# Token halves for the first feature tiles after seven block boundaries of a three-block transformer kernel

## The chip, the core and the metric

The kernel runs on one core of one Trainium2 chip, as one program. The metric is the device time of one execution in microseconds (us). Times of the trace are counted from the start of the span, the time from the first to the last instruction.

## The reference

Two blocks of a first model and one of a second run one after the other over x of 512 tokens by 1024 features, all in float32. What matters here is where a block's parts meet:

```
for i in range(2):
    m = even_mixer(x) if i % 2 == 0 else odd_mixer(x)      # attention
    x = layer_norm(ALPHA * x + m, ln1_g[i], ln1_b[i])
    x = layer_norm(ALPHA * x + square(relu(x @ w_up[i])) @ w_down[i], ln2_g[i], ln2_b[i])
    x = x + sigmoid(x @ ple_w_gate[i] + ple_b_gate[i]) * (p[i] @ ple_w_proj[i])
h = rmsnorm(x, norm1_g)                                    # gated linear attention, convolution
x = x + mixed(h)
h2 = rmsnorm(x, norm2_g)
x = x + (silu(h2 @ w_ffn_gate) * (h2 @ w_ffn_up)) @ w_ffn_down
return rmsnorm(x, norm_f_g)
```

## The kernel before, in words

**Products.** Every float32 product is made of three products of rounded parts (type fp32r): high by high, high by low, low by high (`mm3`). Weights come as 301 chunks of 128 x 1024, in the order of `STAGES`. SP loads a chunk into RW (four buffers). POOL's `cut` makes its high part WH (L532) and then its low part WL (L535), in two buffers each, when TensorE has used the chunk two before (`chunk_used`). TensorE waits for `lo_split` before it uses a chunk. The activations lie with features on partitions as 8 tiles k of 128 x 512 tokens: XTH (high) and XTL (low).

**Order of the work.** Each engine runs one list written by hand, and semaphores join the lists. A projection runs over k = 0 to 7 outermost (two k to a chunk); in `features` each k has 4 column groups of 3 matmuls of 512 columns, into four PSUM banks.

**Boundaries.** Eight places, b = 0 to 7, stand where a block's part ends and a norm (or, at b = 2, nothing but the sum) comes between it and the next projection. `BOUND[b]` is (residual is added, kind of norm, number of its gains). Boundaries 0, 1, 3, 4 are "layer", 6 and 7 are "rms" with an addition, 2 has no norm and 5 is "rms" without an addition, these two behind an embedding stage. At a boundary with an addition four token tiles t of 128 x 1024 go through:

- VectorE (DVE, `boundary`): residual(t) (L1588 or L1593, from PSUM), then scale(t-1) one tile later: reciprocal L1599, then L1605 (layer) or L1609 (rms). Its order is residual 0, 1, scale 0, residual 2, scale 1, residual 3, scale 2, scale 3.
- ScalarE (ACT, `boundary`): deviation(t), the squares L2107 or L2110 and the root L2111; then copy_out(t), L2118, which brings the turned tile from PSUM to YT (in the profile: HT), the last tile in two halves of features; then gain and bias for k = 1 to 7 (L2139, L2142) over all 512 tokens.
- TensorE (PE, `boundary`): 8 transposes (L894) of each tile; between them `occupy` fills waits with matmuls on a tile of ones whose results nobody reads.
- DVE again: for each k over all 512 tokens the gain and bias of k = 0 (L1629, L1632), the high part (L1637) and the low part (L1638), which counts `xt_ready`; after the last k the residual tiles get gain and bias (L1572, L1573).

TensorE then starts the next projection at k = 0: `hidden` (boundaries 0, 3, 6), `embedding` and its `gate_half` (1, 4), or `features` (2, 5). At 1 and 4 `embed_tile`, a product that needs nothing of the norm, is run between the transposes.

**Other places touched.** `forget_sums` (L1200 and L1201): four float32 matmuls of 512 columns into one bank. The last boundary, b = 7: scale is L1613, and SP stores each tile of out by one DMA of 512 KB (L519). Some operands of the third block (QIH to STL, GLH, TWH, OH and their low parts) start 128 or 192 bytes behind a multiple of 256 bytes in a partition, which follows from the sizes of what is placed before them.

Of the kernel before, what the change touches and what calls it, by code (L numbers as in the profile page):

```python
# [81 lines left out]
FOX0 = 16  # L82

# [91 lines left out]
def program(nc, d, out):  # L175
    ctx = ExitStack()
    with ctx:
# [19 lines left out]
        IDLE = sb("IDLE", [P, P], F32R)  # L197
        EPS = sb("EPS", [P, 2])
# [28 lines left out]
        _pad = sb("PAD_PREPARE", [P, 8], at=prepare)  # L227
# [76 lines left out]
        _pad = sb("PAD_THIRD", [P, 8], at=third)  # L304
# [19 lines left out]
        DEC = sb("DEC", [P, 2, NCH], at=third)  # L324
        ST = sb("ST", [P, 2, 2 * DV], at=third)
# [6 lines left out]
        ORS = sb("ORS", [P, GLA_H], at=third)  # L332
        decays = ExitStack()
# [24 lines left out]
        def turned_at(b, t):  # L358


            return (t if BOUND[b][0] else (t + 2) % T) * D

        def probs(h):
# [121 lines left out]
                 (True, "layer", 3), (False, "rms", 4), (True, "rms", 5), (True, "rms", 6)]  # L485
        Y_BASE = [0, 4, 8, 12, 16, 20, 20, 20]

        @block.sync
        def _(sp):
# [30 lines left out]
            sp.wait_ge(out_stored, 16 * T)  # L520
# [3 lines left out]
        def _(pool):  # L524
            own = Order(pool, pool_own)

            def cut(i, j):
# [6 lines left out]
                pool.wait_ge(hi_split, 2 * (j + 1) + 2 * RAW * i)  # L534
                pool.tensor_tensor(WL[:, j % WS, :], RW[:, j % RAW, :], WH[:, j % WS, :].bitcast(F32),  # L535
# [76 lines left out]
            over_chunks(pool, FIRST["out0"] + WS - 1, c + 3, cut)  # L612
# [27 lines left out]
            over_chunks(pool, FIRST["out1"] + WS - 1, CHUNKS, cut)  # L640
# [3 lines left out]
        def _(pe):  # L644
# [20 lines left out]
            def features(c, bank, r=0, new=0, freed=None, late=None, steps=None):  # L665
# [4 lines left out]
                for k in range(k_tiles):  # L670
                    cc, u = c + k // 2, UNIT * (k % 2)
                    if new:
                        pe.wait_ge(xt_ready, KD * (new - 1) + k + 1)
                    if k % 2 == 0:
                        chunk(cc, r)
                    for m, col in enumerate(columns):
                        if freed is not None and k == 0:
                            pe.wait_ge(mix_out, freed + m + 1)
                        if late is not None and k == 0 and m == 3:
                            pe.wait_ge(yt_copied, late)  # L680
# [9 lines left out]
            def tokens(c, bank, h=XTH, l=XTL, k_tiles=KD, new=0, steps=None, freed=None):  # L690

                for k in range(k_tiles):
                    cc, u = c + k // 2, UNIT * (k % 2)
                    if new:
# [214 lines left out]
            def hidden(c, groups, g0, new):  # L909
# [8 lines left out]
                for g in range(n):  # L918
                    one(g, 0)
# [1480 lines left out]
```

## Time and profile before

| | us |
|---|---|
| median of 3 runs | 1978.86 (1978.25 to 1979.53) |
| the profiled execution, its own time | 1978.09 |
| its span | 1976.3 |
| mean granted TensorE clock | 0.998 |
| busy: PE, PEld | 1947.2, 1616.1 |
| busy: POOL, DVE, ACT | 1261.1, 868.8, 327.0 |

PE is TensorE's matmuls, PEld its weight loads, which overlap them. The profiled execution's time is 1.8 us above its span and 0.8 us below the median. Fill matmuls (`occupy`, operand IDLE) count as busy PE: 152 records, 42.4 us.

### The profile page before, as it was taken

How to read it: one execution, taken by the hardware profiler on the slowest of the kernel's cores; microseconds unless marked ns; L12 is line 12 of the kernel's file. 1: busy time of each engine (PE TensorE's matmuls, PEld its weight loads, DVE VectorE, ACT ScalarE, POOL GpSimd, SP SyncE). 2: the span in 40 equal slices, each digit the busy share in tenths (PEclk: the TensorE clock that was granted, in tenths of full speed). 3: DMA queues.
4: the chain of work that ended last, by engine and by line, in shares of the span. 5: the costliest groups of instructions: out<-in, count | busy, mean ns of one | idle time of the engine just before them, and what ended most of it. 6: DMA issues, size and time to landing. Idle time of an engine off the chain costs nothing.

```text
span 1976.3 us, 24552 instructions
## 1 busy us (share of the span) xinstructions
PE 1947.2 (99%) x9180; PEld 1616.1 (82%) x9180; DVE 868.8 (44%) x1208; ACT 327.0 (17%) x627; POOL 1261.1 (64%) x818
## 2 busy tenths in 40 slices
PE   9999999999999999999999999999999999999998
PEld 8788788888887878888788888877888788888886
DVE  3587372253349511472832343377457840000234
ACT  1377300000003100462300000033122130000001
POOL 5586576667767547775566677756453556666674
PEclk9999999999999999999999999999999999999999
DMA  6410233333332323112233333322222233333332
GB/s 225 131 33 33 85 107 96 96 96 117 96 96 85 97 69 108 60 54 79 72 121 99 99 116 98 96 84 88 67 86 65 75 94 98 96 96 96 96 96 75
DMA packets 53698, 181.31 MB, mean 92 GB/s; under 512 B 6584, under 2 KB 9322, under 8 KB 53498
## 3 DMA queue, kind: packets, MB, share of 16 engines
q1 hardware_dynamic: 46656, 165.17, 26.8%
q10 hardware_dynamic: 6970, 15.11, 2.2%
q8 instruction: 53, 0.87, 0.2%
q14 instruction: 19, 0.16, 0.0%
HBM read 176.56 MB, written 3.70 MB: 91 GB/s over the span
## 4 chain that ended last, share of the span: by engine, by line
PE 90%; DVE 4%; POOL 3%; ACT 1%; issue 1%; POOLq 0%; DVEq 0%
PE PS L646 87%; POOL WL L535 1%; PE PS L815 1%; PE PS L894 1%; POOL WH L532 1%; POOL PB L563 1%; DVE STL L1871 0%; DVE X L1605 0%; DVE PS L1588 0%; DVE STH L1870 0%; DVE ST L1880 0%; DVE U L1933 0%; ACT HT L2107 0%; ACT PTH L2058 0%; DVE PTL L1518 0%
## 5 line engine op out<-in xcount | busy, mean ns | idle before, releaser
L535 POOL TENSOR_TENSOR WL<-RW,WH 128x1024 fp32r<-128x1024 f32 x301 | 762.7, 2534 | 25.1
L532 POOL TENSOR_SCALAR WH<-RW 128x1024 fp32r<-128x1024 f32 x301 | 351.7, 1169 | 628.0 <-PE PS L646 603.5
L646 PE MATMUL PS<-XTH,WH 128*128 128x512 f32 x1168 | 457.3, 392 | 2.1 <-DVE XTL L1638 1.6
L646 PE MATMUL PS<-XTL,WH 128*128 128x512 f32 x1168 | 455.4, 390 | 0.0
L646 PE MATMUL PS<-XTH,WL 128*128 128x512 f32 x1168 | 455.3, 390 | 0.0
L646 PE MATMUL PS<-WL,HSH 128*128 128x512 f32 x688 | 267.6, 390 | 2.1 <-POOL WL L535 2.1
L646 PE MATMUL PS<-WH,HSL 128*128 128x512 f32 x688 | 267.7, 389 | 0.0
L646 PE MATMUL PS<-WH,HSH 128*128 128x512 f32 x688 | 267.6, 389 | 0.0
L646 PEld LDWEIGHTS PS<-XTH,WH 128*128 128x128 f32 x1168 | 219.7, 188 | 50.9 <-DVE XTL L1638 3.7
L646 PEld LDWEIGHTS PS<-XTH,WL 128*128 128x128 f32 x1168 | 219.7, 188 | 45.9
L646 PEld LDWEIGHTS PS<-XTL,WH 128*128 128x128 f32 x1168 | 219.6, 188 | 44.0
L646 PE MATMUL PS<-WH,XTH 128*128 128x512 f32 (+1 forms) x480 | 182.7, 385 | 1.5 <-POOL WL L535 0.9
L646 PE MATMUL PS<-WL,XTH 128*128 128x512 f32 (+1 forms) x480 | 181.3, 383 | 0.5 <-POOL WL L535 0.5
L646 PE MATMUL PS<-WH,XTL 128*128 128x512 f32 (+1 forms) x480 | 181.6, 382 | 0.0
L1691 DVE CAST HSH<-HT 128x512 fp32r (+1 forms) x86 | 40.3, 468 | 273.8 <-PE PS L646 273.0
L646 PEld LDWEIGHTS PS<-WL,HSH 128*128 128x128 f32 x688 | 128.9, 188 | 30.0 <-POOL WL L535 3.4
L646 PEld LDWEIGHTS PS<-WH,HSL 128*128 128x128 f32 x688 | 129.2, 188 | 26.9
L646 PEld LDWEIGHTS PS<-WH,HSH 128*128 128x128 f32 x688 | 129.2, 188 | 26.8
L1653 DVE TENSOR_SCALAR HT<-PS 128x2048 f32 (+1 forms) x16 | 36.7, 2292 | 202.2 <-PE PS L646 201.5
L1692 DVE TENSOR_TENSOR HSL<-HT,HSH 128x512 fp32r<-128x512 f32 x86 | 124.0, 1442 | 3.0
L646 PEld LDWEIGHTS PS<-WH,XTH 128*128 128x128 f32 x480 | 90.0, 188 | 22.2 <-issue 4.6
L1675 DVE TENSOR_TENSOR HT<-PS,GT 128x1024 f32 (+1 forms) x11 | 13.5, 1225 | 214.7 <-ACT GT L2270 214.7
(337 smaller groups left out, 2304.7 us busy)
## 6 DMA issues: line engine op xcount, KB each, us to landing
RW<-stream SPq DMA_DIRECT2D x302, 512.0 KB, 3.6
BC<-gate_rows SPq DMA_DIRECT2D x16, 256.0 KB, 3.2
G<-gain_rows ACTq DMA_DIRECT2D x5, 512.0 KB, 3.7
X<-x ACTq DMA_DIRECT2D x1, 2048.0 KB, 11.1
G<-bias_vecs ACTq DMA_DIRECT2D x4, 512.0 KB, 5.2
out<-X SPq DMA_DIRECT2D x4, 512.0 KB, 2.7
XS<-xt ACTq DMA_DIRECT2D x3, 512.0 KB, 8.3
bias_rows<-QM ACTq DMA_DIRECT2D x1, 1536.0 KB, 6.8
```

The source lines that it names most:

```text
L532: pool.tensor_scalar(WH[:, j % WS, :], RW[:, j % RAW, :], 1.0, 1.0, ALU.mult, ALU.mult).then_inc(hi_split, 1)
L535: pool.tensor_tensor(WL[:, j % WS, :], RW[:, j % RAW, :], WH[:, j % WS, :].bitcast(F32), ALU.subtract).then_inc(lo_split, 1)
L563: x = pool.tensor_scalar(p, p, SM[:, s, i:i + 1], 1.0, ALU.mult, ALU.mult)
L646: return pe.matmul(o, a, b, start=start, stop=stop)
L815: x = pe.transpose(PSF[:, o:o + P], probs(h)[:, p:p + P], IDENT[:, :])
L894: x = pe.transpose(PSF[:, o:o + P], src[:, k * P:(k + 1) * P], IDENT[:, :])
L1653: ve.tensor_scalar(h, PS[:, 4 * (g % 2):4 * (g % 2) + 4, :], 0.0, None, MAX).then_inc(relued, 1)
L1675: ve.tensor_tensor(h, PS[:, bank + 2:bank + 4, :], GT[:, :, :], M).then_inc(relued, 1)
L1691: own(ve.tensor_copy(HSH[:, k % 2, :], h))
L1692: ve.tensor_tensor(HSL[:, k % 2, :], h, HSH[:, k % 2, :].bitcast(F32), SUB).then_inc(hs_ready, 1)
```

## The change

It touches all seven boundaries before b = 7, that last one, and the places of some operands:

- The first three feature tiles (k = 0, 1, 2) behind a boundary are made in two halves of 256 tokens. TensorE begins with the half of tokens 0 to 255 before token tile 3 is normed; it turns tile 3 between these products. The four banks are first set to zero by a matmul with a tile of zeros (`clear`), and all products add to them. (`gate_half` needs no `clear`, since its token tiles have banks of their own.)
- ScalarE, not VectorE, makes the high part of k = 3 to 7 at boundaries with a norm.
- VectorE's scale(3) comes after the first half's splits: after all three, at "rms" after two, and after one at boundaries 1 and 4.
- POOL's low part of the second chunk behind a boundary waits until VectorE has made the third tile's first half. ScalarE copies out tiles 0 and 1 before deviation(3).
- Of the fill matmuls three stay at boundaries with an addition and no embedding, eight at b = 5.
- At b = 0, 3, 5, 7 a root of a spare element is taken by ScalarE before the first deviation. The last tile of out is scaled and stored in two halves.
- In `forget_sums` the columns that are zero are left out: 512, 384, 256 and 128 columns.
- Pads put the operands of the third block on multiples of 256 bytes.

```diff
+SPLIT_K = 3
+HALVES = (slice(0, S // 2), slice(S // 2, S))
+def ready_parts(b, k, half):
+    base = KD + (KD + SPLIT_K) * b
+    return base + (half * SPLIT_K + k + 1 if k < SPLIT_K else SPLIT_K + k + 1)
...
-        _pad = sb("PAD_THIRD", [P, 8], at=third)
+        _pad = sb("PAD_U", [P, 40], at=third)
...
+        _pad = sb("PAD_DEC", [P, 48], at=third)
...
+        _pad = sb("PAD_ORS", [P, 16], at=third)
...
-            return (t if BOUND[b][0] else (t + 2) % T) * D
+            return (t if BOUND[b][0] else t % 2 + 2) * D
...
-            for t in range(T):
-                sp.wait_ge(y_ready, Y_BASE[7] + t + 1)
-                sp.dma_start(out[:, t, :], X[:, t, :]).then_inc(out_stored, 16)
+            ends = [(t, slice(0, D)) for t in range(T - 1)] + [(T - 1, half) for half in OUT_HALVES]
+            for j, (t, w) in enumerate(ends):
+                sp.wait_ge(y_ready, Y_BASE[7] + j + 1)
+                sp.dma_start(out[:, t, w], X[:, t, w]).then_inc(out_stored, 16)
...
                 pool.wait_ge(hi_split, 2 * (j + 1) + 2 * RAW * i)
+                if b is not None:
+                    pool.wait_ge(xt_ready, ready_parts(b, SPLIT_K - 1, 0))
                 pool.tensor_tensor(WL[:, j % WS, :], RW[:, j % RAW, :], WH[:, j % WS, :].bitcast(F32),
...
+            cut_stages(FIRST["out0"] + WS - 1, ((0, "up0"), (1, "ple0"), (2, "fox")), c + 3)
...
+            cut_stages(FIRST["out1"] + WS - 1, ((3, "up1"), (4, "ple1"), (5, "gla"), (6, "ffn")), CHUNKS)
...
+            def clear(bank):
+                mm(PS[:, bank, :].rearrange("p (t n) -> p t n", t=T), ZERO[:, :],
+                   IDLE[:, :].unsqueeze(1).to_broadcast([P, T, P]), True, False)
+            def first_group(c, b, turn_tile):
+                def one(k, half):
...
+                    pe.wait_ge(xt_ready, ready_parts(b, k, half or 0))
+                    for m in range(4):
+                        w = slice(u + m * P, u + (m + 1) * P)
+                        x = mm3(PS[:, m, ts], WH[:, cc % WS, w], WL[:, cc % WS, w],
+                                XTH[:, k, ts], XTL[:, k, ts], False, k == KD - 1)
+                    return x
+                chunk(c)
+                one(0, 0)
+                if not BOUND[b][0]:
+                    turn_tile(T - 1)
+                one(1, 0)
+                if BOUND[b][0]:
+                    turn_tile(T - 1)
+                chunk(c + 1)
+                one(2, 0)
+                one(0, 1)
+                one(1, 1).then_inc(chunk_used, 1)
+                one(2, 1)
+                for k in range(SPLIT_K, KD):
...
             def boundary(b, c, embed=None):
                 add, kind, n = BOUND[b]
                 if kind and not add:
                     pe.wait_ge(emb_z, 16)
                     occupy(4, 8)
+                    pe.wait_ge(var_ready, 4 * n + T)
+                    for bank in range(T):
+                        clear(bank)
+                turn_tile(b, 0)
+                turn_tile(b, 1)
                 if embed:
+                    pe.wait_ge(yt_copied, 5 * b + 1)
+                    embed(0)
+                    embed(1)
+                    turn_tile(b, 2)
+                    pe.wait_ge(yt_copied, 5 * b + 2)
+                    embed(2)
+                    turn_tile(b, T - 1)
+                    embed(3)
+                    return
+                if add:
+                    pe.wait_ge(yt_copied, 5 * b + 1)
+                    occupy(0, 3)
+                elif not kind:
+                    pe.wait_ge(y_ready, Y_BASE[b] + T)
...
+                turn_tile(b, 2)
+                first_group(c, b, lambda t: turn_tile(b, t))
...
                for t in range(T):
-                    mm(PS[0:RANK, 4, :], LF[:, RANK * t:RANK * (t + 1)],
-                       STEPS[:, 3 * P - t * P:3 * P - t * P + S], t == 0, t == T - 1)
+                    mm(PS[0:RANK, 4, t * P:], LF[:, RANK * t:RANK * (t + 1)],
+                       STEPS[:, 3 * P:3 * P + S - t * P], t == 0, t == T - 1)
...
+                    last_at = 1 if embedding_layer is not None else 2 if kind == "rms" else SPLIT_K
+                    for k in range(SPLIT_K + 1):
+                        if kind and add and k == last_at:
+                            scale(3)
+                        if k < SPLIT_K:
+                            split_half(k, 0)
+                    for k in range(SPLIT_K):
+                        split_half(k, 1)
+                    for k in range(SPLIT_K, KD):
...
+                        split(k)
...
+                if kind and b in (0, 3, 5, 7):
+                    act.activation(SPARE[:, 0:1], EPS[:, 0:1], F.Sqrt)
+                ahead = T if b == 7 or not add else T - 1
+                if kind:
+                    for t in range(ahead):
+                        deviation(t)
+                if b < 7:
+                    copy_out(0)
+                    copy_out(1)
+                if kind and ahead < T:
+                    deviation(T - 1)
...
+                        for k in range(1, SPLIT_K):
+                            features_ready(k, HALVES[0])
+                    copy_out(2)
                     copy_out(T - 1, slice(0, KD // 2))
...
+                        for k in range(1, SPLIT_K):
+                            features_ready(k, HALVES[1])
+                        features_ready(SPLIT_K)
+                    copy_out(T - 1, slice(KD // 2, KD))
...
+                        for k in range(SPLIT_K + 1, KD):
+                            features_ready(k)
```

`split(k, ts)` is the old work of one k on DVE (k = 0: gain and bias; the high part where k < 3 or at b = 2; the low part), over the tokens ts; `features_ready(k, ts)` is ACT's gain and bias and, from k = 3 on, its copy into XTH. The old loops that these replace are gone.

## Rows read from the trace of the kernel before

**Rows 1.** The page: busy time by engine, and the chain by engine.
```profile
PE 1947.2 (99%) x9180; PEld 1616.1 (82%) x9180; DVE 868.8 (44%) x1208; ACT 327.0 (17%) x627; POOL 1261.1 (64%) x818
...
PE 90%; DVE 4%; POOL 3%; ACT 1%; issue 1%; POOLq 0%; DVEq 0%
```

**Rows 2.** Windows, boundaries 0, 1, 2, 5, 6: last product to next (columns: first row).
```profile
core 0: us, PE busy (x) PEld busy (x) DVE busy (x) ACT busy (x) POOL busy (x), PEclk, DMA share, GB/s
234.20:244.35 10.15, 8.41 (x50) 6.26 (x49) 7.95 (x16) 8.15 (x13) 5.71 (x3) 1.00 0.32 103
594.00:605.46 11.46, 11.14 (x64) 8.79 (x62) 8.69 (x15) 9.59 (x16) 5.72 (x4) 1.00 0.29 92
655.70:661.73 6.03, 5.74 (x41) 5.06 (x42) 3.06 (x6) 3.82 (x5) 3.42 (x2) 1.00 0.37 110
...
1371.70:1385.66 13.96, 11.36 (x65) 9.17 (x65) 8.42 (x15) 10.68 (x18) 3.42 (x2) 1.00 0.20 70
1598.60:1607.19 8.59, 8.04 (x53) 6.49 (x50) 6.59 (x9) 6.86 (x12) 6.89 (x4) 1.00 0.25 67
```

**Rows 3.** Timeline of boundary 0: start us, us, engine, line, operation [idle before].
```profile
230.23 1.28 ACT L2111 ACT_TABLE_LOAD   x1
...
239.41 1.34 DVE L1605 TENSOR_SCALAR X<-PS,MV,RSTD 128x1024 f32<-128x1024 f32 x1
...
241.94 0.59 ACT L2118 COPY HT<-PS 128x512 f32<-128x512 f32 x1 [0.68 <-PE PS L894]
242.56 0.82 ACT L2139 ACTIVATE HT<-HT,BIASES,GAINS 128x512 f32<-128x512 f32 x1
242.56 0.55 DVE L1629 TENSOR_SCALAR HT<-HT,GAINS,BIASES 128x512 f32<-128x512 f32 x1 [1.81 <-ACT HT L2118]
243.14 0.43 DVE L1637 CAST XTH<-HT 128x512 fp32r<-128x512 f32 x1
...
243.60 0.69 DVE L1638 TENSOR_TENSOR XTL<-HT,XTH 128x512 fp32r<-128x512 f32 x1
```

**Rows 4.** Timeline of TensorE (PE) in the third block: matmuls of 256 columns.
```profile
1487.20 0.28 PE L646 MATMUL PS<-STL,QEH 128*128 128x256 f32 x1
1487.32 0.28 PE L646 MATMUL PS<-STH,QEL 128*128 128x256 f32 x1
```

**Rows 5.** Timeline behind boundary 1: POOL's and DVE's low parts side by side.
```profile
606.58 2.44 POOL L535 TENSOR_TENSOR WL<-RW,WH 128x1024 fp32r<-128x1024 f32 x1
606.81 2.76 DVE L1638 TENSOR_TENSOR XTL<-HT,XTH 128x512 fp32r<-128x512 f32 x1
```

**Rows 6.** Timeline of boundary 5.
```profile
1373.09 2.37 POOL L535 TENSOR_TENSOR WL<-RW,WH 128x1024 fp32r<-128x1024 f32 x1
1373.69 2.32 DVE L1715 TENSOR_SCALAR HT<-X,RSTD 128x1024 f32<-128x1024 f32 x1
...
1376.07 1.09 PE L894 MATMUL PS<-IDENT,HT 128*128 128x128 f32 x8 [2.18 <-DVE HT L1715]
```

**Rows 7.** Timeline of the last boundary: the table load, the root behind it, the last scale.
```profile
1963.18 1.28 ACT L2111 ACT_TABLE_LOAD   x1
1964.48 0.29 ACT L2111 ACTIVATE STD<-MV,EPS 128x1 f32<-128x1 f32 x1
...
1971.68 1.28 DVE L1613 SCALAR_TENSOR_TENSOR X<-X,RSTD,G 128x1024 f32<-128x1024 f32 x1
```

**Rows 8.** The page: the four stores of out.
```profile
out<-X SPq DMA_DIRECT2D x4, 512.0 KB, 2.7
```

**Rows 9.** Timeline of TensorE (PE): forget_sums.
```profile
722.37 3.61 PE L646 MATMUL PS<-STEPS,LF 128*16 128x512 f32 x8
```

**Rows 10.** Windows of products: inside a projection, with OH, with XTH (columns as rows 2).
```profile
300.00:334.00 34.00, 34.00 (x152) 28.16 (x151) 7.71 (x3) 0.00 (x0) 22.06 (x14) 1.00 0.31 100
...
1557.96:1574.56 16.60, 16.60 (x71) 13.49 (x72) 16.36 (x13) 1.96 (x4) 11.20 (x6) 1.00 0.30 95
1576.20:1590.00 13.80, 13.80 (x62) 11.43 (x61) 2.00 (x3) 0.62 (x1) 9.78 (x6) 1.00 0.36 112
```

More of the change, by code:

```diff
@@ L972, in one @@
                                k == 0, k == KD - 1)
-                for k in range(KD - 2):
-                    if new:
-                        pe.wait_ge(xt_ready, KD * (new - 1) + k + 1)
+                if b is not None:
+                    pe.wait_ge(yt_copied, 5 * b + 3)
+                    for half in range(2):
+                        if half:
+                            pe.wait_ge(yt_copied, 5 * b + 5)
+                        for k in range(SPLIT_K):
+                            if k % 2 == 0 and not half:
+                                chunk(c + k // 2)
+                            pe.wait_ge(xt_ready, ready_parts(b, k, half))
+                            for t in (2 * half, 2 * half + 1):
+                                x = one(k, t)
+                            if k == 1 and half:
+                                x.then_inc(chunk_used, 1)
+                for k in range(0 if b is None else SPLIT_K, KD - 2):
+                    if b is not None:
+                        pe.wait_ge(xt_ready, ready_parts(b, k, 0))
                     if k % 2 == 0:
@@ L984, in gate_half @@
                         x.then_inc(chunk_used, 1)
[L985 to L986 removed]
+                if b is not None:
+                    pe.wait_ge(xt_ready, ready_parts(b, KD - 1, 0))
                 chunk(c + 3)
@@ new lines, in split @@
+                def split(k, ts=slice(0, S)):
+                    y = YT[:, k, ts]
+                    if k == 0 and layer:
+                        own(ve.tensor_scalar(y, y, GAINS[:, n, 0:1], BIASES[:, n, 0:1], M, A))
+                    elif k == 0 and kind:
+                        own(ve.tensor_scalar(y, y, GAINS[:, n, 0:1], None, M))
+                    if k < SPLIT_K or not kind:
+                        own(ve.tensor_copy(XTH[:, k, ts], y))
+                    ve.tensor_tensor(XTL[:, k, ts], y, XTH[:, k, ts].bitcast(F32), SUB).then_inc(xt_ready, 1)
@@ new lines, in split_half @@
+                def split_half(k, half):
+                    if k and kind:
+                        ve.wait_ge(yt_ready, (KD + SPLIT_K - 2) * n + (SPLIT_K - 1) * half + k)
+                    else:
+                        ve.wait_ge(yt_copied, 5 * b + 2 + 2 * half)
+                    split(k, HALVES[half])
+                if kind:
+                    residual(0)
+                    residual(1)
+                    if add:
+                        scale(0)
+                    residual(2)
+                    if add:
+                        scale(1)
+                    residual(3)
+                    if add:
+                        scale(2)
+                    if b == 7 or not add:
+                        scale(3)
```

196 lines of the change are left out of this document (87 added, 109 removed).

## The prediction

> **What bounds the kernel now.** I read the page first. TensorE is busy for 99% of the span and POOL, the next, for 64%; the chain that ended last runs through TensorE for 90% [rows 1]. So an edit pays only where TensorE waits, fills, or multiplies what need not be multiplied. Those places are the boundaries. In windows from the last product of one part to the first of the next, 10.15 us pass at boundary 0, 11.46 at 1, 6.03 at 2, 13.96 at 5 and 8.59 at 6 [rows 2]; 3 goes like 0 (10.09) and 4 like 1 (11.45). The busy time in those windows is mostly fill, transposes (four times 1.09 [rows 6]) and, at 1 and 4, the embedding product. The timeline of boundary 0 says which wait ends last: scale 3 on DVE (1.34), transposes, half a copy (0.59), gain (0.55), high part (0.43), low part (0.69) [rows 3], and the first product starts at 244.35. All of tile 3 has to pass before any product starts. At boundary 5 two more things show: a DVE scale that took 2.32 beside POOL's low part of 2.37, and TensorE idle for 2.18 until it was done [rows 6].
>
> **Prices.** Half a feature tile on DVE: the whole takes 0.55, 0.43 and 0.69 [rows 3]; a half costs at least half of that and at most all. I take 0.35, 0.28 and 0.42, near the lower end, since length sets most of such an operation. So k = 0 costs 1.15 with gaps, k = 1 and 2 cost 0.75 each. ACT's half gain: 0.5 of 0.82 [rows 3]. ACT's high part of 512 columns: never seen here; between the copy's 0.59 and the gain's 0.82 [rows 3], I take 0.62. Products of 256 columns: two starts lie 0.12 us apart [rows 4], 0.115 over a longer stretch, against 0.227 for 512 columns (34.00 us for 150 of them, two of the 152 counted lying across the edges [rows 10]); twice the weight loads cost next to nothing (72 half products a boundary, 0.1 to 0.2). Twelve such products, one k of one half, are 1.4 us. `clear` and the three fills take 0.23 each in time in which TensorE waits anyway.
>
> **Boundaries 0 and 3.** The table load of 1.28 stands between the squares of tile 0 and their root [rows 3]; scale 0 waits for it, and residual 2 and all that follows on DVE stand behind scale 0. With the root taken ahead, in idle time of ACT, I put 1.15 of it on the path (0 if something else held DVE; at most 1.28). Scale 2, which ended a little before scale 3's 239.41, would then end near 238.0. New order: DVE's first half of k = 0 until 239.15, k = 1 until 240.1 (behind deviation 3 on ACT), k = 2 until 240.9; TensorE starts at 239.2, 5.1 earlier than now. Then it waits for more: scale 3 ends at 242.4, tile 3 is turned by 243.4; POOL's low part of the second chunk, released at 240.9, takes 2.4 and ends at 243.3; k = 2, first half, runs until 244.8; the copy, gain and split of the second half of k = 0 are done at 245.2. So TensorE waits about 0.4, and the three k end at 249.4. Now the same 36 products of 0.227 end at 252.5. Gain 3.1 each. Later k are covered: ACT needs about 1.5 for a k (gain, then high part), TensorE 2.7. The next cut of POOL is released earlier than now (second half of k = 1, at 248.0) and is needed at 252.1.
>
> **A rule against the trace.** ACT starts its next instruction 1.30 after the load's start [rows 7], so a removed load is worth at most 1.3 here. The Trainium skill, ScalarE: Activation LUTs, section What ACT_TABLE_LOAD costs, adds a drain and makes a switch 2.66 us; by that page the three loads on the path (b = 0, 3, 7) would give some 4 us more. No row shows the drain, and my sum goes by 1.3.
>
> **Boundaries 1 and 4.** The table is loaded already. Half 0 is split at about 601.9, since scale 3 comes after its first k. But here the second chunk is the first that `gate_half` uses: TensorE can't start before POOL's low part ends, 601.9 + 2.4 = 604.3, against 605.46. Then POOL cuts the next chunk at once (until 607.9), TensorE needs it at 607.1 for k = 2, and DVE's second half is caught beside it: an operation of 0.69 became 2.76 beside POOL's 2.44 [rows 5]. Start 1.1 earlier, stall 0.8: gain 0.2 each, bounds -1.5 and +1.1.
>
> **Boundary 2.** No norm. TensorE begins after two copies instead of four, 659.9 instead of 661.73, turns tile 3 (1.1) in between, and waits for POOL from the first half's 661.4 until 663.8. End of the three k: 669.4 against 669.9. Gain 0.5.
>
> **Boundary 5.** POOL's low part, which now held DVE from 1373.69 to 1376.01 [rows 6], comes after the splits: four scales of 0.8 end at 1377.1. The fills between the turns go, and turns 0 to 2 need no deviation beside them. ACT finishes its deviations at 1376.1 (load gone), copies 0 and 1 by 1378.15; first product at 1379.35 against 1385.66. Turn of tile 3, POOL until 1383.25, second half ready by 1384.4: the three k end at 1388.8 against 1393.9. Gain 5.1, the largest term; bounds 3 (DVE's halves locked behind POOL once) and 6.
>
> **Boundary 6.** No load here, and the first chunk's cut still holds scale 2. First product at 1603.95 against 1607.19, POOL until 1608.9, end 1614.5 against 1615.4. Gain 0.9.
>
> **The end.** The load of 1.28 [rows 7] holds scale 0 and so residuals 2 and 3: 0.9 of it counts, as tile 3's sums are then the limit. Last scale 1.28 [rows 7]: two halves of about 0.68. A store of 512 KB takes 2.7 to land [rows 8]; of 256 KB, started 0.1 later than the old one relative to the scale, I take 2.0 (bounds 1.4 and 2.7). Gain 0.9 + 0.6, with less queueing behind tile 2's store: 1.7, bounds 0.9 and 2.3.
>
> **Sums, places, start.** The four float32 matmuls of 2048 columns take about 3.55 until the next group [rows 9]; 1280 columns take 2.2: gain 1.3, as TensorE is bound there. The 72 products with OH start 0.234 apart, those with XTH behind them 0.230 and elsewhere 0.227 [rows 10]. If the place of the operand is the reason, 96 products with OH and 24 with TWH give 0.4 to 0.8: I take 0.6, bounds 0 and 1.5, since smaller operands may gain too. The memset of ZERO stands behind that of IDLE, and TensorE waits for both before its first fill: 0.1 lost. The DMAs on ACT's queue (forget and gate weights) start with the last `xt_ready` as before; they have no new wait. DVE's gains and biases of the residual start no later than now.
>
> **Sum.** 2 x 3.1 + 2 x 0.2 + 0.5 + 5.1 + 0.9 = 13.1; with 1.7, 1.3, 0.6 and -0.1: 16.6. The profiled execution, 1978.1, goes to 1961.5; it stands 0.8 below the median, so the median goes from 1978.9 to **1962.3**.
>
> **Rivals.**
> 1. *The head start is given back.* TensorE starts early and then stands before the second half, because scale 3, turn, copy and split of tile 3 are now behind more work. Against it: I find only 0.4 of such waiting. For it: DVE has 2.2 of half splits ahead of scale 3 at boundaries 0 and 3. Then boundaries 0 and 3 give only the load (1.2 each), 5 gives 3.5, 6 and 2 nothing: 5.9, with the 3.5 of other terms 9.4. Time 1969.5. Chance 0.16.
> 2. *POOL's new wait becomes the bound.* The low part of 2.4 [rows 6] is released by DVE and awaited by TensorE, with slack near zero at all seven; half of it, 1.2, lost at each is 8.4. Time 1970.7. Chance 0.12.
> 3. *Slower: the clock falls.* Some 120 fill matmuls go, and TensorE waits uncovered for up to 1 us several times in a boundary. For it: less activity. Against it: it stood idle for 2.18 at boundary 5 [rows 6] in a window whose granted clock is 1.00 [rows 2]. At the lower level (1.2 instead of 2.4 GHz) each product of 0.227 takes as much again; it becomes slower overall from 16.6 / 7 = 2.4 us a boundary, some 11 products at the low level after each. At 20 products, 4.5 x 7 = 32 lost: 1994. Chance 0.03. The Trainium skill, TensorE: Matmul & The Clock Gate, section HAM oscillation, says that gaps between bursts of matmuls can bring the clock down again and again; by that rule this case would come about, and no row of this kernel has shown it so far.
> 4. *The change doesn't do what it says* (both 1 and 2, the load still in the path, places without effect): 1 to 4 gained, about 1976. Chance 0.07.
>
> **How the numbers follow.** My forecast has 0.62. Its own terms leave 1958 to 1966. The range takes rivals 1 and 2 in and leaves out 3 and 4: 1957 to 1971. A measurement of this kernel can tell about 0.2%, 4 us, from no change: faster is the forecast and rivals 1 and 2 (0.90), less what may fall short, 0.89; same 0.08; slower 0.03.
>
> **What would show it.** Right: no table load between squares and root at boundaries 0, 3 and 7; first product near 239.3 at boundary 0 and a group of 12 matmuls of 256 columns 0.115 apart; TensorE's wait for DVE's second half at most 0.5; at boundary 5 scales of 0.75, none of 2.3; the low part of POOL ending when k = 1 and turn 3 end. Wrong: idle before TensorE's k = 2 with POOL L535 as releaser, over 1 us; DVE's half splits of over 1 us beside POOL; products 0.4 apart behind a boundary, or a granted clock below 0.99.

## The result, and the profile after

The changed kernel took 1963.76 us (median of 4, 1961.73 to 1965.80) beside 1978.55 for the kernel before (median of 4, 1978.11 to 1979.53): ratio 0.9924, 95% interval 0.9912 to 0.9936, 14.8 us faster. Forecast were 1962.3 and a range of 1957 to 1971. The profiled execution took 1963.95, its span is 1962.0 against 1976.3.

Page of the changed kernel, busy time by engine, beside [rows 1]:

```profile
PE 1932.6 (99%) x9287; PEld 1612.3 (82%) x9287; DVE 869.2 (44%) x1228; ACT 349.7 (18%) x673; POOL 1262.0 (64%) x818
```

TensorE's busy time fell by 14.6, all but 0.3 of which shows in the span (14.3). ACT took over 22.7 us of work, DVE's hardly changed: the high parts went, the gaps and locks of halves came.

Windows from the last product of one part to the first of the next, boundaries 0, 1, 2, 5, 6 of the changed kernel, as [rows 2]:

```profile
core 0: us, PE busy (x) PEld busy (x) DVE busy (x) ACT busy (x) POOL busy (x), PEclk, DMA share, GB/s
233.91:238.75 4.84, 4.70 (x31) 3.65 (x30) 4.55 (x9) 4.72 (x10) 3.35 (x2) 1.00 0.27 69
591.05:601.30 10.25, 9.45 (x57) 7.61 (x55) 8.34 (x16) 7.92 (x15) 5.73 (x4) 1.00 0.14 51
652.80:657.14 4.34, 3.75 (x30) 3.34 (x29) 2.76 (x6) 2.18 (x3) 1.04 (x1) 1.00 0.27 101
1365.34:1372.70 7.36, 5.82 (x36) 4.78 (x37) 6.40 (x15) 7.23 (x15) 1.07 (x1) 1.00 0.13 52
1586.73:1592.03 5.30, 4.51 (x32) 3.71 (x30) 5.16 (x7) 4.41 (x9) 4.14 (x3) 1.00 0.24 65
```

The first product comes 5.3, 1.2, 1.7, 6.6 and 3.3 us sooner. That isn't the gain: token tile 3 is now turned behind the first product, and new waits may lie there. So I measure stretches instead, from the start of the last product ahead of one boundary to that ahead of the next (the last one to the end of the span). Each holds one boundary with all that it drags behind it:

| stretch, us | before | after | gain | forecast |
|---|---|---|---|---|
| boundary 0 to 1 | 359.76 | 357.14 | 2.6 | 3.1 |
| 1 to 2 | 61.75 | 61.76 | 0.0 | 0.2 |
| 2 to 3 (with forget_sums) | 294.05 | 292.60 | 1.5 | 0.5 + 1.3 |
| 3 to 4 | 360.24 | 357.07 | 3.2 | 3.1 |
| 4 to 5 | 61.69 | 62.87 | -1.2 | 0.2 |
| 5 to 6 (with OH, TWH) | 226.95 | 221.39 | 5.6 | 5.1 + 0.6 |
| 6 to the end | 378.08 | 375.66 | 2.4 | 0.9 + 1.7 |

Two of the seven, 1 and 4, gave nothing or lost. Now the timelines, beginning with boundary 0 of the changed kernel (engines merged, by start):

```profile
236.15 1.34 DVE L1693 TENSOR_SCALAR X<-PS,MV,RSTD 128x1024 f32<-128x1024 f32 x1
237.41 0.41 DVE L1713 TENSOR_SCALAR HT<-HT,GAINS,BIASES 128x256 f32<-128x256 f32 x1
237.85 0.29 DVE L1717 CAST XTH<-HT 128x256 fp32r<-128x256 f32 x1
238.18 0.43 DVE L1718 TENSOR_TENSOR XTL<-HT,XTH 128x256 fp32r<-128x256 f32 x1
...
240.38 2.39 POOL L556 TENSOR_TENSOR WL<-RW,WH 128x1024 fp32r<-128x1024 f32 x1 [3.12 <-DVE XTL L1718]
241.74 1.09 PE L946 MATMUL PS<-IDENT,X 128*128 128x128 f32 x8
244.75 0.39 PE L677 MATMUL PS<-XTH,WH 128*128 128x256 f32 x1 [0.24 <-DVE XTL L1718]
...
245.32 0.62 ACT L2247 CAST XTH<-HT 128x512 fp32r<-128x512 f32 x1
```

A half costs 0.41, 0.29 and 0.43, where 0.35, 0.28 and 0.42 were taken; ACT's high part costs 0.62, as taken. TensorE starts at 238.75 and waits 0.24 for the second half. POOL's low part stands right behind the first half's last split. On DVE only scale 3 runs beside it, which reads PSUM: it takes 1.35 there (from 240.34), as it does with POOL idle (1.34, in the run without POOL's wait below). The scale of boundary 5, which reads SBUF, was the one that took 2.32.

Boundary 5, beside [rows 6]: no scale of 2.32 any more, and POOL's low part starts 3.3 us behind the last scale's end:

```profile
1367.37 0.75 DVE L1832 TENSOR_SCALAR HT<-X,RSTD 128x1024 f32<-128x1024 f32 x1
...
1369.95 0.75 DVE L1697 TENSOR_SCALAR HT<-X,RSTD 128x1024 f32<-128x1024 f32 x1
1372.70 0.36 PE L677 MATMUL PS<-XTH,WH 128*128 128x256 f32 x1 [1.03 <-DVE XTL L1718]
1374.04 2.39 POOL L556 TENSOR_TENSOR WL<-RW,WH 128x1024 fp32r<-128x1024 f32 x1 [7.35 <-DVE XTL L1718]
```

Boundary 1, where nothing was won: DVE and POOL, and TensorE's wait for each chunk:

```profile
601.33 1.14 DVE L1717 CAST XTH<-HT 128x256 fp32r<-128x256 f32 x1
602.41 2.38 POOL L556 TENSOR_TENSOR WL<-RW,WH 128x1024 fp32r<-128x1024 f32 x1
602.51 2.57 DVE L1718 TENSOR_TENSOR XTL<-HT,XTH 128x256 fp32r<-128x256 f32 x1
...
609.44 1.05 POOL L550 TENSOR_SCALAR WH<-RW 128x1024 fp32r<-128x1024 f32 x1 [4.64 <-PE PS L677]
609.48 2.09 DVE L1660 TENSOR_TENSOR X<-X,G 128x1024 f32<-128x1024 f32 x1
610.58 3.23 POOL L556 TENSOR_TENSOR WL<-RW,WH 128x1024 fp32r<-128x1024 f32 x1
```

POOL's second low part makes the chunk for k = 2 ready at 604.79: TensorE's wait there is 0.57 (forecast 0.8). But POOL's next cut begins only when k = 1 of both halves is multiplied, 609.44, and by then DVE has the residual's gain and bias (L1660, L1661). The low part takes 3.23, and TensorE waits 0.63 more, for k = 4. At boundary 4 the same two waits are 0.77 and 1.47:

```profile
1320.91 1.22 DVE L1660 TENSOR_TENSOR X<-X,G 128x1024 f32<-128x1024 f32 x1
1321.13 1.91 POOL L550 TENSOR_SCALAR WH<-RW 128x1024 fp32r<-128x1024 f32 x1 [4.67 <-PE PS L677]
1322.16 1.95 DVE L1661 TENSOR_TENSOR X<-X,G 128x1024 f32<-128x1024 f32 x1
1323.13 3.21 POOL L556 TENSOR_TENSOR WL<-RW,WH 128x1024 fp32r<-128x1024 f32 x1
```

The end, beside [rows 7]: no table load, the last residual starts 0.04 behind TensorE's last product, and the two halves of the last scale take 1.41. From that product's end (1954.90) to the end of the span it is 7.1; before it was 8.7.

```profile
1954.94 1.22 DVE L1681 SCALAR_TENSOR_TENSOR X<-X,PS 128x1024 f32<-128x1024 f32 x1
1957.37 0.29 ACT L2228 ACTIVATE STD<-MV,EPS 128x1 f32<-128x1 f32 x1
1957.90 1.41 DVE L1702 SCALAR_TENSOR_TENSOR X<-X,RSTD,G 128x512 f32<-128x512 f32 x2
```

Products with OH in the changed kernel, 72 in 16.46 where [rows 10] have 71 in 16.60; over all 96 the starts within a run lie 0.2273 apart, before 0.2325:

```profile
1546.54:1563.00 16.46, 16.46 (x72) 13.62 (x73) 16.21 (x13) 1.96 (x4) 11.51 (x6) 1.00 0.33 96
```

### The profile page after: what moved, and what is told of

Read it like the earlier page. It is cut to its first block and busy times, and to the rows that moved or that the text cites. A ratio compares the mean times of both kernels' runs of the same rounds, so it can differ in the third digit from the quotient of the medians.

```text
span 1962.0 us, 24847 instructions
## 1 busy us (share of the span) xinstructions
PE 1932.6 (99%) x9287; PEld 1612.3 (82%) x9287; DVE 869.2 (44%) x1228; ACT 349.7 (18%) x673; POOL 1262.0 (64%) x818
## 5 line engine op out<-in xcount | busy, mean ns | idle before, releaser
L677 PE MATMUL PS<-XTH,WH 128*128 128x512 f32 (+1 forms) x1228 | 469.1, 382 | 3.9 <-DVE XTL L1718 2.3
L677 PE MATMUL PS<-XTH,WL 128*128 128x512 f32 (+1 forms) x1228 | 466.0, 379 | 0.0
L677 PE MATMUL PS<-XTL,WH 128*128 128x512 f32 (+1 forms) x1228 | 465.9, 379 | 0.0
L677 PEld LDWEIGHTS PS<-XTH,WH 128*128 128x128 f32 x1228 | 231.3, 188 | 51.3 <-POOL WL L556 3.8
L677 PEld LDWEIGHTS PS<-XTH,WL 128*128 128x128 f32 x1228 | 231.2, 188 | 43.6
L677 PEld LDWEIGHTS PS<-XTL,WH 128*128 128x128 f32 x1228 | 231.4, 188 | 42.1
```

Source lines behind the costliest of these rows:

```text
L677: return pe.matmul(o, a, b, start=start, stop=stop)
```

## The experiments

Twelve runs were made, each beside the kernel before, the first of them with the changed kernel itself. Where no other is named, the measure for a time is the changed kernel at 1963.6 to 1963.8.

**The changed kernel again** (no edit), to learn how far its stretches repeat.

> The changed kernel once more, on the chip that also runs the next three. Theory: 1963.8 us again, and the stretch from the last product before boundary 4 to the last before boundary 5 takes 62.9 us again, with two waits for POOL's low part (0.77 and 1.47 us), since DVE's gain and bias of the residual (0.8 us apart from the next cut in the first trace) slow POOL's third cut. Rival: that stretch was a chance of one execution and is 61.8 us, as at boundary 1, in this one.

Measured: 1963.61 (1961.78 to 1964.84), ratio 0.9925 (0.9908 to 0.9941). The stretch behind boundary 4 is 62.88 again, with the same two waits (0.79 and 1.52), as the theory had it. Six of the seven stretches agree within 0.13 with the first profile. The seventh, 2 to 3, is 290.97 instead of 292.60; the clock section below tells why.

**Without the spare root ahead**, at b = 0, 3, 5, 7:

```diff
-                if kind and b in (0, 3, 5, 7):
-                    act.activation(SPARE[:, 0:1], EPS[:, 0:1], F.Sqrt)
```

> The changed kernel without the root of a spare element taken ahead, so that the table load of 1.28 us is back behind the first squares of boundaries 0, 3 and 7. Theory (the load delays scale 0 and all that stands behind it on DVE): first products of boundaries 0 and 3 come 1.1 to 1.2 us later, the end 0.9 us later, together 3.2 us slower than the changed kernel. Rival A (the halves hide it): less than 1 us. Rival B (a switch costs 2.66 us by the Trainium skill, ScalarE: Activation LUTs, section What ACT_TABLE_LOAD costs): 7 us.

**Only the root ahead**, the same two lines added to the kernel before:

> The kernel before, with one edit: the spare root ahead at b = 0, 3, 5, 7. Theory (a table load between squares and root delays scale 0 by 1.2 wherever ACT's deviations lead): boundaries 0 and 3 give 1.2 each, the end 0.9, 3.3 together, and boundary 5 nothing, since there DVE's scale of 2.32 beside POOL ends last: 1975.3. Rival A (at boundary 5 too, as in the changed kernel, where leaving the root out cost 1.2): 4.5 faster, 1974.1. Rival B (the load was hidden at 0 and 3 in the kernel before, and only the new order brings it onto the path): 0.9 faster, 1977.7.

Measured: without it 1969.64 (1967.05 to 1970.87), ratio 0.9955 (0.9938 to 0.9971), 6.0 slower, nearly twice the 3.2 of the theory. The stretches behind 0, 3 and 5 grow by 1.4, 1.2 and 1.2, the end by 1.1, which makes 4.9 (boundary 5 was not in the theory); 1.1 more is behind boundary 1, where POOL is caught for longer. So the total comes near Rival B's 7, but no single place shows its 2.66. Alone on the kernel before it gave 1974.56 (1972.29 to 1976.21), ratio 0.9976 (0.9964 to 0.9987), 4.3 faster: 1.3 at 0, 1.3 at 3, 1.4 at the end (4.0 together) and nothing at 5 (227.01 against 226.95). So a load is on the path wherever ACT leads, at 1.1 to 1.4 each. At boundary 5 of the kernel before it was hidden by the locked DVE scale, which is there still:

```profile
1371.47 2.32 DVE L1716 TENSOR_SCALAR HT<-X,RSTD 128x1024 f32<-128x1024 f32 x1
```

Once POOL's low part is out of its way, the load would be late there too: the two edits share that gain. The timeline of ACT without the root, boundary 0:

```profile
230.34 1.28 ACT L2228 ACT_TABLE_LOAD   x1
231.63 0.29 ACT L2228 ACTIVATE STD<-MV,EPS 128x1 f32<-128x1 f32 x1
```

The next instruction starts 1.29 behind the load's start. The Trainium skill, ScalarE: Activation LUTs, section What ACT_TABLE_LOAD costs, has 1283 ns for the load, as here, and a drain that makes the switch 2.66 us. The trace doesn't show the drain in this place, and four places of at most 1.4 speak against it.

**POOL's low part not held back**, at any boundary:

```diff
-                if b is not None:
-                    pool.wait_ge(xt_ready, ready_parts(b, SPLIT_K - 1, 0))
```

> The changed kernel without POOL's wait for DVE's first half before the low part of the second chunk, at all seven boundaries. Theory (DVE and POOL exclude each other, so the low part must not lie in DVE's splits): at boundary 5 a scale of 2.3 us instead of 0.75 returns and the first product comes 1.3 to 1.6 us later; at 0 and 3 the low part ends at about 239 instead of 242.8 and holds DVE's first half by 1.3 to 2 us, so that the first product is 1.5 us later, and about 0.5 us of it is won back at the third feature tile; at 1 and 4 nothing, as the low part ends before the embedding product does in either case. Sum 2 to 4 us slower. Rival (POOL's wait is the new bound): 2 to 5 us faster, since TensorE no longer waits for the second chunk.

Measured: 1975.86 (1973.73 to 1978.12), ratio 0.9986 (0.9977 to 0.9996): 12 slower, three times what I expected. At boundary 0 POOL's low part now starts 0.09 before DVE's first half, and DVE stands:

```profile
237.43 2.37 POOL L553 TENSOR_TENSOR WL<-RW,WH 128x1024 fp32r<-128x1024 f32 x1
237.52 2.42 DVE L1710 TENSOR_SCALAR HT<-HT,GAINS,BIASES 128x256 f32<-128x256 f32 x1
```

0.41 became 2.42, and all that follows on DVE is 2.0 late: the stretches grow by 1.9 at 0, 1.9 at 1, 3.4 at 3, 0.8 at 4, 1.4 at 5 and 2.0 at 6. This one wait of POOL carries most of what the change brings. At boundary 3 a fall of the clock is in it: TensorE stands for 2.14, and the windows around and behind that have the clock at 0.73 and 0.92. But at boundary 6 of the same execution it stands for 2.65, its longest wait at a boundary, and the clock stays at 1.00:

```profile
956.56 0.36 PE L674 MATMUL PS<-XTH,WH 128*128 128x256 f32 x1 [2.14 <-DVE XTL L1715]
...
1604.01 0.36 PE L674 MATMUL PS<-XTH,WH 128*128 128x256 f32 x1 [2.65 <-DVE XTL L1715]
```

```profile
955.00:960.00 5.00, 3.44 (x19) 3.47 (x20) 4.02 (x9) 0.90 (x1) 0.48 (x1) 0.73 0.39 117
960.00:965.00 5.00, 4.52 (x35) 4.31 (x35) 2.18 (x7) 2.87 (x5) 0.00 (x0) 0.92 0.00 0
1604.00:1610.00 6.00, 5.57 (x45) 5.37 (x46) 3.22 (x10) 1.95 (x4) 0.00 (x0) 1.00 0.23 87
```

Back to the two rows of boundary 0. The Trainium skill, SBUF — State Buffer, section SBUF: two separate sides, says that the ports which VectorE's faster operations, or those with two SBUF inputs, share with GpSimd are an exclusive lock: whoever starts first has them for the whole instruction, and the other blocks. The rows agree: DVE ends at 239.94, 0.14 after POOL's 239.80, and POOL is not slowed (2.37), rather than both going at half speed.

**DVE makes the high parts again** for k = 3 to 7, ACT only the gains:

```diff
-                    if k < SPLIT_K or not kind:
-                        own(ve.tensor_copy(XTH[:, k, ts], y))
+                    own(ve.tensor_copy(XTH[:, k, ts], y))
```

> The changed kernel, but DVE makes the high part of k = 3 to 7 again, ACT only the gains. Theory (that part of the change gives nothing by itself: DVE needs 0.43 + 0.69 = 1.1 us for a k, ACT 0.8, and TensorE 2.7): 0 plus or minus 0.5, 1963.6. Rival A (DVE's high parts push its low parts into POOL's cuts, where 0.69 becomes 2.76, and the next k is late): idle of TensorE before k = 3 or 4 of up to 1 us at boundaries 0, 3, 5 and 6, 2 to 4 us slower, 1966 to 1968. Rival B (ACT's gain followed by its high part and an extra pass is the slower way, and k = 3 comes sooner without): up to 1 us faster.

Measured: 1964.12 (1963.29 to 1964.62), ratio 0.9925 (0.9909 to 0.9942): no difference, as the theory had it. The stretches of boundaries 0, 3, 5 and 6 are within 0.25 of those of the changed kernel. At 1 and 4 the wait for k = 4 is gone, since DVE comes later to the residual, and another comes further on: TensorE stands 1.17 and 1.69 for DVE's embedding work (tile SG).

**Without the last fills** at boundaries 0, 3, 5, 6:

```diff
-                    occupy(4, 8)
...
-                    occupy(0, 3)
```

> The changed kernel without the fill matmuls that are left at the boundaries (three at 0, 3, 6, eight at 5), so that TensorE waits with nothing to do. Theory (the waits there don't bring the clock down): the granted clock at every boundary stays 1.00, products behind it 0.115 and 0.227 apart, 0 plus or minus 0.3 us, 1963.6. Rival (the fills are what holds the clock): a granted clock of 0.5 in a stretch behind boundary 5, or behind 0 and 3 as well, with products twice as far apart; 20 such products cost 2.3 to 4.5 us a boundary, 1966 to 1980.

Measured: 1965.96 (1963.05 to 1966.16), ratio 0.993 (0.9913 to 0.9946). The boundaries are the same to 0.1 (stretches 357.21, 357.16, 221.42, 375.52), at a granted clock of 1.00 in all of them, though TensorE now stands for 2.06 at boundary 5. That the median is 2 higher isn't from there: in the profile 1.1 is boundary 1 (62.86 instead of 61.8) and 1.6 the fall of the clock behind forget_sums.

**The three small parts undone**: forget_sums, pads and last store as before (the three pads are put back as well):

```diff
-                    mm(PS[0:RANK, 4, t * P:], LF[:, RANK * t:RANK * (t + 1)],
-                       STEPS[:, 3 * P:3 * P + S - t * P], t == 0, t == T - 1)
+                    mm(PS[0:RANK, 4, :], LF[:, RANK * t:RANK * (t + 1)],
+                       STEPS[:, 3 * P - t * P:3 * P - t * P + S], t == 0, t == T - 1)
...
-        OUT_HALVES = (slice(0, UNIT), slice(UNIT, D))
+        OUT_HALVES = (slice(0, D),)
```

> The changed kernel with its three small parts outside the halves undone: forget_sums over 512 columns in all four matmuls, the pads as before, the last tile of out scaled and stored whole. The trace of the changed kernel shows the 96 products with OH at 0.2273 us apart instead of 0.2325 and the 24 with TWH at 0.2270 instead of 0.2326 (0.6 us together), and a span that ends 7.1 us behind the last product instead of 8.7. Theory (each small part is worth what its rows say): 1.3 (sums) + 0.6 (places) + 0.6 (last store) = 2.5 us slower, 1966.1; the stretch from boundary 2 to 3 longer by 1.3, that from 5 to 6 by 0.6, with the pitch of OH back at 0.232 to 0.234. Rival A (the place of the operand has nothing to do with the pitch, which came from something beside it): pitch stays at 0.227, 1.9 slower. Rival B (the last store is hidden behind that of tile 2): the end keeps its 7.1, again about 1.9 slower, told apart from A by the stretch.

Measured: 1965.76 (1965.31 to 1968.30), ratio 0.9932 (0.9916 to 0.9949), 2.0 to 2.2 slower. The stretch 2 to 3 grows by 1.2. The OH products go back to 0.2325 apart, the TWH ones too (from 0.227 to 0.2327), on the same data and beside the same work, so the place is the reason; by pitch that is 0.6, though the stretch 5 to 6 shows only 0.4. The end behind the last product grows from 7.1 to 7.3: within the span the last store in halves is worth 0.3, not the 0.6 I had put. Outside it, the time stands 2.3 to 2.4 above the span in all four executions of this kernel, beside 1.8 to 2.0 in those of every other; no trace shows why.

**Another order of the gate product** at boundaries 1 and 4: k = 0 and 1 of both halves, and then k = 2, so that the first chunk is freed before k = 2 begins:

```diff
-                    for half in range(2):
-                        if half:
+                    for k, half in ((0, 0), (1, 0), (0, 1), (1, 1), (2, 0), (2, 1)):
+                        if k == 0 and half:
```

> The changed kernel with another order of the first gate products at boundaries 1 and 4: both halves of k = 0 and 1, then both of k = 2, so that the first gate chunk is used up before the next is begun. Theory (the halves' order asks for the second gate chunk 2.7 us after the start instead of 5.4, and frees the first 1.4 us later, so that the third chunk's cut falls into DVE's gain and bias): the waits for POOL (0.57 and 0.63 at boundary 1, 0.77 and 1.47 at 4) go, and one wait of about 1.1 us for DVE's second half comes; boundary 1 within 0.3 us, boundary 4 1.0 us faster; sum 1.0 us. Rival (POOL is slow there whatever the order, as DVE's gain and bias run beside it): no difference.

Measured: 1959.88 (1959.03 to 1962.33), ratio 0.9905 (0.9888 to 0.9921), 3.8 faster. The stretches are 60.37 (from 61.8) and 61.70 (from 62.9). At boundary 1 all waits for POOL behind the first product are gone; at boundary 4 one of 0.95 is left, for DVE:

```profile
1313.48 2.40 POOL L556 TENSOR_TENSOR WL<-RW,WH 128x1024 fp32r<-128x1024 f32 x1
1313.58 2.58 DVE L1717 TENSOR_TENSOR XTL<-HT,XTH 128x256 fp32r<-128x256 f32 x1
```

POOL came 0.10 ahead of DVE, and the second half of k = 0 was late. At boundary 1 of the same execution DVE's same part began first (602.78, POOL's at 603.73) and ended at 603.92; the lock then fell on the next k's high part (2.50), for which nobody waited. Which of the two is first differs between boundaries and executions of one kernel: in the combined version below boundary 1 has the wait and 4 has not. The two stretches make 2.6 of the 3.8; for the rest no place shows. Part of it may be the clock: three of these four executions have a mean granted clock of 0.999, but only four of the eight of the changed kernel.

**The same order, and POOL free at boundaries 1 and 4:**

```diff
-            cut_stages(FIRST["out0"] + WS - 1, ((0, "up0"), (1, "ple0"), (2, "fox")), c + 3)
+            cut_stages(FIRST["out0"] + WS - 1, ((0, "up0"), (2, "fox")), c + 3)
...
-            cut_stages(FIRST["out1"] + WS - 1, ((3, "up1"), (4, "ple1"), (5, "gla"), (6, "ffn")), CHUNKS)
+            cut_stages(FIRST["out1"] + WS - 1, ((3, "up1"), (5, "gla"), (6, "ffn")), CHUNKS)
```

> The version with the new order of the gate product (k0 and k1 of both halves first), and POOL's low part behind boundaries 1 and 4 not held back any more. Theory (POOL's wait earns its time there too, since a free low part lies beside DVE's scale or first half split): the first product of the gate comes 0.8 later as in the run without any such wait, at 1 and 4 each, 1.6 us slower than the new order alone: 1961.5. Rival (with the new order the wait only delays POOL, whose low part ends last before the first product there): 0.5 faster at each, 1958.9.

Measured: 1959.45 (1958.95 to 1960.07), ratio 0.9902 (0.9887 to 0.9917). The theory had it 1.6 slower, the rival 1.0 faster; it is neither. The first product comes 0.8 later, as the theory said (DVE's first half takes 2.45 beside POOL's 2.40), but both stretches are 60.8, as the mean of 60.4 and 61.7 nearly is: what is lost at the start comes back as waits that don't arise later. At 1 and 4 POOL's wait is worth nothing; it belongs to boundaries where a head start can be kept.

**No token halves in the gate product:**

```diff
-                    for half in range(2):
-                        if half:
-                            pe.wait_ge(yt_copied, 5 * b + 5)
...
+                    pe.wait_ge(yt_copied, 5 * b + 5)
...
+                        for t in range(T):
```

> The changed kernel, but at boundaries 1 and 4 the gate product takes k = 0 to 2 over all 512 tokens, when both halves are ready (DVE still makes them in halves). Theory (halves start TensorE 1.3 earlier there, and it all went back into waits for POOL): first product about 1.5 to 2.5 later than in the changed kernel, no wait for POOL behind it, and the stretch from boundary 1 to 2 within 0.5 of 61.8, so the total 1963.6 plus or minus 1. Rival (without halves it would be worse than the kernel before, as DVE now works in halves with scale 3 between): stretch of 63.5 or more, 1966 to 1968.

Measured: 1969.71 (1965.62 to 1970.47), ratio 0.9954 (0.9939 to 0.9969), 6 slower, above both the theory and the rival. The stretch behind boundary 1 is 62.1, only 0.3 more than with halves, which is the theory. Behind boundary 4 it is 65.5: POOL's cut caught DVE's split, TensorE stood for 4.20, and then the clock fell to 0.50, which is the lower level of 1.2 GHz. A wait of 2.30 at boundary 1 of the same execution left it at 1.00. The profiled execution is the fastest of the four, so what the others lost is in no profile; two of them took 1970.4 at a mean granted clock of 0.997, lower than that of the one with the fall, 0.999. Timeline of TensorE, and the windows behind the wait:

```profile
1315.75 0.47 PE L677 MATMUL PS<-WH,XTH 128*128 128x512 f32 x1 [4.20 <-DVE XTL L1716]
...
1317.00 0.63 PE L677 MATMUL PS<-WL,XTH 128*128 128x512 f32 x1
1317.43 0.63 PE L677 MATMUL PS<-WH,XTL 128*128 128x512 f32 x1
```

```profile
1315.60:1317.00 1.40, 1.25 (x4) 1.01 (x5) 1.33 (x6) 1.37 (x3) 0.00 (x0) 0.80 0.50 56
1317.00:1319.00 2.00, 2.00 (x6) 1.63 (x5) 2.00 (x4) 1.94 (x4) 0.00 (x0) 0.50 0.55 223
```

**The clock behind forget_sums.** Windows of the kernel before and of the changed kernel, behind the last 20 matmuls (of 16 columns) of forget_sums:

```profile
728.00:730.00 2.00, 2.00 (x9) 1.66 (x9) 0.81 (x2) 0.58 (x1) 0.00 (x0) 0.79 0.59 217
730.00:732.00 2.00, 2.00 (x6) 1.59 (x5) 0.00 (x0) 0.70 (x1) 0.00 (x0) 0.50 0.05 12
```

```profile
726.00:728.00 2.00, 2.00 (x6) 1.62 (x5) 0.00 (x0) 0.33 (x1) 0.00 (x0) 0.50 0.13 43
723.80:741.00 17.20, 17.20 (x71) 14.04 (x71) 3.10 (x3) 1.28 (x1) 6.90 (x4) 0.90 0.22 63
```

and of the changed kernel measured again, at the same place behind those 20 matmuls as the last window:

```profile
724.65:741.85 17.20, 17.20 (x78) 14.22 (x78) 3.10 (x3) 1.28 (x1) 7.29 (x5) 1.00 0.28 79
```

71 matmuls instead of 78 in 17.2 us, 7 of 0.227 fewer: the fall costs 1.6 (292.60 against 290.97). It shows in seven of the first ten profiles, in the kernel before too. TensorE never stops there; it runs short matmuls. To see whether they are the cause I ran them in two pieces between full products:

```diff
-            features(chunk0 + 8, 0, steps=[[], [(forget_sums, 0)], [], []])
+            features(chunk0 + 8, 0, steps=[[], [(forget_sums, 0)], [(forget_tokens, 0)], [(forget_tokens, 1)]])
```

> The changed kernel, with the 16-column matmuls of forget_sums (20 records, 2.3 us in one piece) taken out of their place and run in two pieces of 6 and 14, each 5.4 us later than the one before, between products of 512 columns. In seven of ten profiles so far the granted clock is 0.50 for 3.4 us right behind that piece. Theory (the piece of short matmuls brings the clock down): the granted clock stays 1.00 there, the stretch from boundary 2 to 3 is 291.0 us as in the profiles without the fall, and the median is 1.2 lower (1.7 in seven of ten): 1962.5; at the end of each wide piece nothing is lost. Rival A (the four wide matmuls with a stationary operand of 16 columns, which stay where they are, do it): the fall comes still, 292.6, in most executions. Rival B (chance of the chip, with no tie to this piece): the fall shows at another place.

Measured: 1962.40 (1962.16 to 1964.28, 5 runs), ratio 0.9919 (0.9906 to 0.9933). The clock stays at 1.00 in the profile, and the mean granted clock is 0.999 in all five executions (it was 0.998 in two of four before). But the stretch is 292.09, not 291.0: TensorE now waits 0.90 for DVE's copy of the sums, which had been covered, so the edit gives back most of what it saves. That the short matmuls are the cause isn't shown by this. The two runs above that leave the piece whole and were made beside this one (POOL free, and no token halves in the gate product) have no fall there in their profiles either, which makes seven in twelve, and the four executions of the one with POOL free all have 0.999. Nor does 0.999 exclude a fall: the profiled execution of the kernel with only the root ahead has that mean, and this very fall in its trace.

**Both edits together:**

> The changed kernel with both edits that looked good: the gate product in the order k0, k1 of the first half, k0, k1 of the second, then k2, and the 16-column matmuls of forget_sums in two pieces. Theory (the two are at places 100 us apart and add up): boundaries 1 and 4 give 1.3 each, the clock 1.2 in the median: 1959.9 less what the fall cost there, 1958.7. Rival (the clock falls anyway, here or elsewhere): 1959.9 to 1960.5.

Measured: 1964.12 (1960.69 to 1964.91, 5 runs), ratio 0.9922 (0.9908 to 0.9936). The profiled execution, 1960.69 with a clock of 1.00 throughout, shows the gain behind boundary 4 (stretch 60.35), while the one behind boundary 1 (61.69) has DVE's wait of 0.95; a second execution took 1961.27. The three executions of 1964 to 1965 have a mean granted clock of 0.997 or 0.998, so the clock fell in them, at a place that no profile shows. What decides it stays open. The best version that ran is the new order of the gate product, with POOL held back there (1959.88) or free (1959.45); the two can't be told apart.

## Why the prediction was right, and where not

- **Boundaries 0, 3, 5, 6, 2** (forecast 3.1, 3.1, 5.1, 0.9, 0.5): right in place and nearly in size. The run with the small parts undone takes them out of the stretches: 5.2 is left at 5 and 0.3 at 2, and at 6 0.9 beside the kernel with only the root ahead. The wait for the second half was put at 0.4 and is 0.24. What no run shows is the share of the halves alone at these five places: the root and POOL's wait were taken away there, the halves never were, and their share is read from the timelines. At 0 the gain is 0.5 short; one wait not in my list is POOL's for the third chunk, 0.34.
- **Boundaries 1 and 4: the step that failed.** It ended with "Start 1.1 earlier, stall 0.8: gain 0.2 each". (1.1 less 0.8 is 0.3; it put 0.2.) The start is 1.27 earlier at boundary 1 and 1.20 at 4, the stall 0.57 and 0.77, both fine. I stopped at k = 2. With the old order of k, POOL gets the next chunk only after k = 1 of the second half, and then works beside the residual's gain and bias: 0.63 and 1.47 more of waiting. That is 1.6 of the 2.3 by which the profile falls short of the forecast's 16.6. Freeing that chunk sooner took 1.4 and 1.2 off the two stretches, which shows the cause.
- **The table load**: 1.15 on the path at 0 and 3; measured 1.2 to 1.4. At 5 it was in the 5.1 as "load gone" and is 1.2 there, but only together with POOL's wait.
- **POOL's wait** was not priced by itself, and my expectation for its removal, 2 to 4, was a third of the 12 measured. It put about 1 each at 0 and 3 (1.9 and 3.4 measured, the 3.4 with a fall of the clock in it) and 1.3 to 1.6 at 5 (1.4), but nothing at 1 and 4, where 1.9 and 0.8 went, and left out 6, where 2.0 went.
- **The end**: 1.7 forecast, 1.6 measured, with the parts wrong in size: load 1.1 to 1.4 (0.9 put), store 0.3 within the span (0.6 put).
- **Sums, places**: 1.3 and 0.6, measured 1.2 and 0.4 to 0.6. That ACT makes the high parts was costed at nothing, and is worth nothing.
- **Rival 1** (head start given back) is what happened at 1 and 4 alone. **Rival 2** (POOL the bound), with its 1.2 at each place: the waits for POOL behind the first product add up to 1.20 at boundary 1 and 2.24 at 4, but are 0.34 at 0 and 3 and 0.64 at 6, so it holds only at 1 and 4. There the sign of it showed too, half splits of DVE of over 1 us beside POOL (1.14 and 2.57). **Rival 3** (clock) came at no boundary of the changed kernel, with or without fills; but "no row of this kernel has shown it so far" was wrong, as the windows behind forget_sums of the kernel before show it. Nor do some 120 fill matmuls go: the traces have 152 of them before and 79 after. Its mechanism exists: in two of the experiments the clock fell at a boundary, behind TensorE's waits of 4.20 and of 2.14. These two agree with the rule of the Trainium skill (TensorE: Matmul & The Clock Gate, section HAM oscillation), that gaps between bursts of matmuls bring the clock down. But waits of 2.65 and 2.12 in the same execution as that of 2.14, of 2.30 in the same as that of 4.20, of 2.18 [rows 6] and of 2.06 without fills left it at 1.00, so the length of the wait alone doesn't decide, and what does stays open. In the two profiles of the changed kernel the longest wait at a boundary is 1.52.

## What to carry to other kernels

Follow each resource past the point where the head start is spent: the chunk that is freed later by a new loop order is paid two chunks on, beside whatever work then runs. When DVE and POOL both read SBUF, the order in which they start decided 2 us here (0.41 against 2.42), so hold the one that has slack with a semaphore, and then check that nobody needs it sooner. Compare stretches between fixed points, not first products: 1.3 earlier was worth 0 here, 5.3 was worth 2.6.

## What was unexpected

- The granted clock fell to 0.50 for 3.4 us while TensorE was never idle, behind 20 matmuls of 16 columns (2.3 us), in seven of the twelve profiles that have them in one piece, at 1.6 us each. The cause is open. It fits the spread between executions: those of the kernel before with a mean clock of 0.999 took 1976.1 to 1977.0, those with 0.997 or 0.998 took 1978.1 to 1980.1.
- A stationary operand (loaded as weights) that starts 128 or 192 bytes behind a multiple of 256 costs 0.005 to 0.006 us for each matmul of 512 columns (0.2325 to 0.2327 against 0.2267 to 0.2274), and setting it straight by pads gives that back.
- The changed kernel, and the variants that leave this place alone, take 61.7 to 61.8 or 62.9 from boundary 1 to 2, and hardly anything between (61.7 to 61.8 or 62.9 from 4 to 5 too). The difference is which of two operations begins first: POOL's high part at 609.44, before DVE's gain at 609.48 (it takes 1.05), or DVE's gain at 1320.91, before POOL's at 1321.13 (it takes 1.91). All twelve such stretches go by it, in the two profiles of the changed kernel and in those without the root, with the small parts undone, without fills and with the sums in two pieces: POOL first by 0.03 to 0.04 in the four short ones, DVE first by 0.14 to 0.22 in the eight long ones. Some 0.2 us decide over 1.1.
